# FFN down-projections: the weight slots of two output chunks interleaved

## What is computed

```python
D_FF = 2816
def conv_ffn(h, w_up, conv_w, conv_b, w_down):
    u = h @ w_up                      # 512 x 1024 by 1024 x 5632
    u = causal_conv3(u) + conv_b
    a, b = u[..., :D_FF], u[..., D_FF:]
    return (jax.nn.silu(a) * b) @ w_down   # 512 x 2816 by 2816 x 1024
x = x + conv_ffn(rms_norm(x, ffn_norm_g[layer]), w_up[layer], ...)
```

## Time and profile before

| | |
|---|---|
| median of three runs | 1828.44 us |
| the profiled execution, its own time | 1827.0 us |
| its span | 1825.1 us |
| PE busy | 1801.2 us, 99% |
| POOL line 1220 (low parts), 136 times | 584.3 us |
| PE line 844 (down-projections), 1056 matmuls | 411.7 us of busy time |
| PE clock granted, mean | 0.998 |

### The profile page before, as it was taken

The page is one execution under the profiler, slowest core; times in us unless marked ns, Lnnn a source line. Parts: engine busy times, 40 slices in busy tenths (PEclk is TensorE's granted clock), DMA queues, the critical chain, the costliest instruction groups (busy, mean ns, idle before and its releaser), DMA issues.

```text
span 1825.1 us, 24602 instructions
## 1 busy us (share of the span) xinstructions
PE 1801.2 (99%) x9595; PEld 1468.0 (80%) x9595; DVE 916.9 (50%) x1300; ACT 733.8 (40%) x970; POOL 681.3 (37%) x227
## 2 busy tenths in 40 slices
PE   9999989999999999999999999999999999999998
PEld 7799868888888887667888888888877788888886
DVE  6366764555552116664555555235227734313564
ACT  5251163555554224653455555222225542221423
POOL 2225834444443442100444443443343344344432
PEclk9999999999999999999999999999999999999999
DMA  8542202322322231110222222323421122332221
GB/s 333 217 139 70 71 1 75 110 92 92 104 88 79 95 122 62 52 54 24 92 103 105 92 92 84 105 95 108 105 69 47 47 92 92 107 103 105 69 71 68
DMA packets 28763, 170.36 MB, mean 93 GB/s; under 512 B 3216, under 2 KB 5520, under 8 KB 12432
## 3 DMA queue, kind: packets, MB, share of 16 engines
q1 hardware_dynamic: 25152, 151.20, 24.2%
q10 hardware_dynamic: 3536, 18.09, 3.0%
HBM read 167.18 MB, written 2.10 MB: 93 GB/s over the span
## 4 chain that ended last, share of the span: by engine, by line
PE 80%; issue 11%; DVE 3%; POOL 3%; ACT 2%; DMA 0%; ACTq 0%; POOLq 0%; DVEq 0%; SPq 0%
PE ps L403 47%; PE ps L844 12%; POOL wlo L1220 3%; PE ps L423 1%; PE ps L1111 1%; PE ps L700 1%; PE ps L425 1%; PE ps L424 1%; PE ps L1094 1%; PE ps L559 1%; PE ps L561 1%; PE ps L560 1%; PE ps L1123 1%; PE ps L1122 1%; PE ps L1121 1%
## 5 line engine op out<-in xcount | busy, mean ns | idle before, releaser
L1220 POOL TENSOR_TENSOR wlo<-wraw,whi 128x2048 fp32r<-128x2048 f32 (+1 forms) x136 | 584.3, 4296 | 963.2 <-ACT whi L1336 939.5
L403 PE MATMUL ps<-hh,whi 128*128 128x512 f32 x1328 | 520.1, 392 | 0.8 <-DVE wq L2481 0.4
L403 PE MATMUL ps<-hh,wlo 128*128 128x512 f32 x1328 | 516.9, 389 | 0.0
L403 PE MATMUL ps<-hl,whi 128*128 128x512 f32 x1328 | 516.8, 389 | 0.0
L1336 ACT ACTIVATE whi<-wraw 128x2048 fp32r<-128x2048 f32 (+3 forms) x147 | 261.3, 1778 | 356.7 <-PE ps L403 285.1
L403 PEld LDWEIGHTS ps<-hh,whi 128*128 128x128 f32 x1328 | 249.3, 188 | 54.7 <-issue 2.5
L403 PEld LDWEIGHTS ps<-hh,wlo 128*128 128x128 f32 x1328 | 249.3, 188 | 52.0
L403 PEld LDWEIGHTS ps<-hl,whi 128*128 128x128 f32 x1328 | 249.4, 188 | 51.8 <-issue 0.5
L2221 DVE SCALAR_TENSOR_TENSOR scr<-ps,vec,scr 128x510 f32<-128x510 f32 (+1 forms) x176 | 120.2, 745 | 93.1 <-ACT scr L1560 93.1
L844 PE MATMUL ps<-gh,whi 128*128 128x512 f32 x352 | 137.7, 391 | 1.3 <-DVE gl L2236 1.3
L844 PE MATMUL ps<-gh,wlo 128*128 128x512 f32 x352 | 137.0, 389 | 0.0
(11 more groups left out here) (488 smaller groups left out, 2836.8 us busy)
## 6 DMA issues: line engine op xcount, KB each, us to landing
wraw<-in_w SPq DMA_DIRECT2D x62, 1024.0 KB, 4.9
wraw<-in_w0b SPq DMA_DIRECT2D x26, 1024.0 KB, 4.9
wraw<-in_w1o SPq DMA_DIRECT2D x26, 1024.0 KB, 4.9
wraw<-in_wd SPq DMA_DIRECT2D x32, 704.0 KB, 4.0
ada<-in_wada ACTq DMA_DIRECT2D x12, 1024.0 KB, 8.5
xtok<-in_x SPq DMA_DIRECT2D x4, 512.0 KB, 7.2
out<-ytok SPq DMA_DIRECT2D x4, 512.0 KB, 4.0
wraw<-in_w SPq DMA_DIRECT2D x3, 576.0 KB, 3.9
```

The source lines that it names most:

```text
L403: last = mm(o, l, r, start=(k == 0 and n == 0), stop=(k == K - 1 and n == 2))
L1220: nc.gpsimd.tensor_tensor(wlo[:, s % 2, 0:wd], wraw[:, s % 2, 0:wd], whi[:, s % 2, 0:wd].bitcast(F32), ALU.subtract).then_inc(lo_ready, 1)
```

## The change

The order of the slots within a pair of output chunks changes. Before: chunk A first half, chunk A second half, chunk B first half, chunk B second half. Now: A first, B first, A second, B second. The weights are laid out for it on the host (`down`). Both PSUM banks are open at once. Chunk A is complete after the third slot of the pair and no longer after the second; chunk B after the fourth, as before. DVE's wait and ACT's conversions are moved to match: `conv_upto(S + 2 * k + 3 - k % 2)` makes the conversion of one slot more before the wait for an even chunk.

```diff
             def down_pair(S_D, layer, i):
-                for n in range(2):
-                    s = S_D + 2 * n
-                    pe.wait_ge(emptied, 4 * i + (s - 2))
-                    for hf in range(2):
-                        pe.wait_ge(lo_ready, 4 * i + (s + hf + 1))
-                        if n == 0 and hf == 1:
+                for hf in range(2):
+                    for n in range(2):
+                        s = S_D + 2 * hf + n
+                        if hf == 0:
+                            pe.wait_ge(emptied, 4 * i + (S_D + 2 * n - 2))
+                        pe.wait_ge(lo_ready, 4 * i + (s + 1))
+                        if hf == 1 and n == 0:
                             pe.wait_ge(f_lo, 22 * layer + 22)
-                        par = (s + hf) % 2
                         for k in range(11):
                             for m, (a, b) in enumerate(((0, 0), (0, 1), (1, 0))):
-                                last = mm(ps[:, 4 + n, :], (whi, wlo)[a][:, par, k * P:(k + 1) * P],
+                                last = mm(ps[:, 4 + n, :], (whi, wlo)[a][:, s % 2, k * P:(k + 1) * P],
...
                     if between:
                         between(k, 0)
-                    conv_upto(S + 2 * k + 2)
+                    conv_upto(S + 2 * k + 3 - k % 2)
                     act.wait_ge(emptied, S + 2 * k + 2)
...
                 for k in range(8):
-                    empty(S + 2 * k + 1)
+                    empty(S + 2 * k + 2 - k % 2)
                     x = xT[:, k, :]
                     TT(x, x, ps[:, 4 + k % 2, :], ALU.add).then_inc(emptied, 2)
...
 def down(wm):
-    return np.ascontiguousarray(wm.reshape(2, 11, P, 8, P).transpose(3, 0, 2, 1, 4).reshape(16, P, DSLOT))
+    return np.ascontiguousarray(wm.reshape(2, 11, P, 4, 2, P).transpose(3, 0, 4, 2, 1, 5).reshape(16, P, DSLOT))
```

## The result

| | before | changed |
|---|---|---|
| median of 15 runs, us | 1827.32 | 1832.15 |
| the profiled execution, us | 1827.0 | 1831.87 |
| its span, us | 1825.1 | 1829.9 |
| PE clock granted, mean | 0.998 | 0.997 |

The ratio is 1.0027, with a 95% interval from 1.0020 to 1.0034. The forecast time, 1831.8, is 0.35 us off, but that closeness is partly luck: the kernel before came out at 1827.32 here, 1.1 us under the 1828.44 that the forecast was added to. The difference is the honest measure: 4.8 us measured, 3.5 forecast, and slower by over 0.2% was given 40%.

The account below looks back on a forecast made before the run. The prediction took TensorE to bound the kernel. Layer 0's +0.5 us and layer 1's +3.0 summed to +3.5, added to the median 1828.44 for a forecast given as 1831.8 us, range 1828.6 to 1834.8.

Parts of the forecast that it names:

- What bounds the kernel: Whole kernel: TensorE bounds it, so a change is worth what it adds to or takes from TensorE's standing time.
- Part 1: Slot 1 of each layer's down-projection: the wait for f_lo goes, gain 1.9 us (1.7 to 2.0).
- Part 2: Layer 0, slots 4 to 15: chunks ending back to back stay covered by 0.5 us before the limit, cost 0.
- Part 3: Layer 0, slot 16: its conversion stands behind chunk 6's work, so its low part is 1.42 us late (1.3 to 1.6).
- E: The start of DVE's addition of a finished chunk, the clock from which conversions and POOL's low parts were timed.
- the limit: E + 7.04: when POOL's low part must be ready; each us past it is one us of TensorE.
- Part 4: Layer 1, context work queued ahead of conversions: slot 8 0.2 us late, slot 12 2.08, slot 16 2.76, net 2.0.
- The three small waits: Layer 1, slots 11, 13 and 15: waits for low parts of weights go, gain 0.3 us.
- One sign: POOL's low part was to become the releaser of the first matmul after each stage: 1.4 us layer 0, 2.8 layer 1.
- The clock: Rival: a long TensorE standstill sends it to 1.2 GHz, +7.5 us each, 1839.4 with one such slot; 4%.
- The cover holds: Rival: waits for `gl` and the small ones go and nothing takes their place, 1826.2 us; 9%.
- partly late: Rival: sooner handovers or downstream waits leave half the lateness, +0.8 us, 1829.2 us; 12%.

Follow-up runs that it names:

- x2: The kernel before with only pair 0 of each down-projection interleaved, pairs 1 to 3 unchanged; lower time 1825.1 us, ratio 0.9991.
- x4: The changed kernel with 11 idle matmuls on TensorE filling the wait ahead of layer 1's slot 16; lower time 1830.15 us, ratio to before 1.0019.
- x6: The changed kernel with layer 1's slot 12 conversion put ahead of chunk 4's square and three context high parts; ratio to before 1.0013.
- x1: The changed kernel with every conversion ahead of the wait for the finished chunk and all chunk and context work; lower time 1825.2 us, ratio 0.9991.
- x7: The changed kernel with layer 1's slot 16 conversion ahead of chunk 6's square and the last two context high parts; lower time 1828.85 us, ratio 1.0012.
- x3: The kernel before in its own slot order, with only the conversions put ahead of the chunk work; lower time 1826.5 us, ratio 0.9998.
- x5: The changed kernel with layer 0's slot 16 conversion put ahead of chunk 6's high part and square; lower time 1830.1 us, ratio to before 1.0020.
- x8: The kernel before with pair 0 alone interleaved and the conversions ahead of the chunk work; median 1824.70 us, lower time 1824.6, ratio 0.9991.

## Why the prediction was right, and the one term that it lacked

- *What bounds the kernel* held for all but the clock. That a change is worth "exactly what it adds to or takes from TensorE's standing time" is true of 3.1 of the 4.8 us; the other 1.7 are TensorE at work at half the clock. Reading the slot from the distance of two additions (7.48 us) and not from the matmuls' durations is what made the lateness visible.
- *Part 1*, the wait for f_lo: 1.9 us forecast, 0.94 and 0.95 in the trace, and 1.9 us alone in x2. Right.
- *Part 2*, back-to-back chunks cost nothing while the cover is 0.5 us: no slot of layer 0 from 4 to 15 waits. Right.
- *Part 3*, slot 16 of layer 0: 1.42 forecast, 1.33 measured, with POOL's end at E + 8.43. Right; by that loss the limit was at E + 7.10 there. The 0.65 us that POOL was said to have ahead of the limit in the kernel before are 0.5 by the working's own figures (677.77 - 0.16 - 677.10); no term rests on it.
- *Part 4*: slot 12, 2.08 forecast and 2.1 measured. Slot 16 until its start, 2.76 and 2.64. The three small waits, 0.3, gone: 0.36 by the starts. Slot 8, 0.2 forecast and 0.25 measured. POOL ended at 1194.52, E + 7.72 with E = 1186.80, 0.07 later than worked out; less the limit of 7.04 and the grace of 0.43 that is the 0.25 us. The times that come back behind slot 16, 0.8, came back. One sign was read off wrongly in advance: the view names not POOL but DVE's `xT` (layer 0) and "issue" (layer 1) for the first matmul of slot 16, and only the starts, 0.1 us behind POOL's ends, tell that it is POOL. Slot 8 in the changed kernel, where it is 1.13 us from slot 7's last matmul to slot 8's second, and 0.89 in the kernel before:

```profile
1193.78 0.39 PE L844 MATMUL ps<-gh,wlo 128*128 128x512 f32 x1
1194.01 0.59 PE L1018 MATMUL ps<-csq,con 128*128 128x256 f32 x2
1194.57 0.50 PE L844 MATMUL ps<-gh,whi 128*128 128x512 f32 x1
1194.91 0.40 PE L844 MATMUL ps<-gl,whi 128*128 128x512 f32 x1
```

- *The clock.* This is the step that failed: the sum put it at nothing, and it cost 1.7 us. That is more than the whole distance between 3.5 and 4.8; the other terms together came out 0.4 us lower than forecast. As a rival I gave it 4% and priced it as a whole slot at half speed, 7.5 us. It fell in the profiled execution after the 2.6 us standstill and not after the one of 2.1, and lasted 3.4 us, which is 1.7 us. Chance and price were both wrong, in opposite directions. The argument against it ("7 us of gapless matmuls on either side") was none: the matmuls ahead of the standstill did not protect it. x4 shows that without the standstill there is no fall; x6, that the standstill alone does not make it certain. A fall with TensorE idle was in the trace of before as well, though in none of the rows: behind its last matmuls the granted clock is 0.80 from 1818 to 1820 us and then 0.50, where nothing is left for it to slow. And of the three times of before one, 1826.79, was 1.7 us under the other two, as one fall would have it. The Trainium skill ("TensorE: Matmul & The Clock Gate", Part 1) has it that activity releases the throttle; by that rule, the trace of x4 agrees, since matmuls that compute nothing of use keep the clock at 1.00.
- *The cover holds* and *partly late* are out: nothing was handed over sooner than worked out.
- DVE held up by POOL played no part in the sum, and rightly: it was off the path in the changed kernel. It decides what the repair is worth. x1 and x7 each lose 0.96 us to it ahead of slot 16, x6 0.4 at slot 13.
- The measured time is inside the stated range, and the terms that were worked out hold to 0.15 us. The range itself does not follow from its parts: the lower and upper ends of the terms add up to +2.5 and +5.4 (stated +2.4 and +5.3), and 1833.7 + 1.4 is 1835.1, not 1834.8. The total came out near 1831.8 because two misses nearly cancel: the change, put 1.3 us too low, and the base, 1.1 us too high. That is luck.

## What to carry to other kernels

An in-order queue that feeds the critical engine must be read as a queue: when a producer's event moves, ask of each instruction behind it in the same queue whether it had been free to run earlier, and add up to the consumer's limit. The reordering that takes a wait away is needed only where the wait is (pair 0), and done everywhere, with the conversions left behind the chunk's work, it cost 4.8 us where pair 0 alone brings 1.9. And where a change makes TensorE stand, add a fall of the clock (1.7 us here) as a case of its own, or fill the wait with idle matmuls. The traces give no length from which on it has to be feared: falls came with waits of 1.1 and 2.6 us, and none with those of 2.1.

## What the runs showed of the hardware

**Two groups of times in every kernel.** In the latent attention, around 820 us, TensorE waits 1.12 us for ACT. In some executions the clock falls there for 3.4 us, in others not. The profiled execution of before (1827.0, lower group) and that of x3 (1828.06, upper group), the same stretch of each:

```profile
820.00:824.00 4.00, 3.28 (x11) 1.43 (x11) 3.69 (x5) 1.21 (x5) 0.00 (x0) 1.00 0.00 0
```

```profile
820.00:824.00 4.00, 3.37 (x5) 1.58 (x6) 3.61 (x5) 1.13 (x4) 0.00 (x0) 0.57 0.00 0
```

The next longer wait, 1.0 us, ends at 827.18, when such a fall is over. The profiled executions of before, x1, x5, x7 and x8 belong to the lower groups and have no fall there; those of x2, x3, x4 and x6 belong to the upper ones and have it. So in the traces the groups are one fall of the clock apart; for the executions without a trace that is inferred from their times. No run filled this wait, so that it is what takes the clock is argued from x4 and not shown.

When the fall begins is not tied to the wait either. In x3 it begins at about 820.2, with TensorE idle until 820.63; in x2 at about 820.6, when TensorE has been back since 819.71. At slot 16 it begins 1.1 us after TensorE resumes in the changed kernel, and in x5 0.25 us before. x5, by stretches:

```profile
1257.00:1257.50 0.50, 0.00 (x0) 0.00 (x0) 0.50 (x1) 0.00 (x0) 0.50 (x1) 1.00 0.00 0
1257.50:1258.00 0.50, 0.29 (x1) 0.32 (x2) 0.50 (x1) 0.00 (x0) 0.11 (x1) 0.54 0.00 0
```

In the changed kernel the fall at slot 16 comes on top in its lower group too; none of its 15 runs is below 1831.6, where one without any fall would be near 1830.1. The same holds for the 9 runs of x5. In x6, whose down stage is 1.7 us shorter up to that place, three runs of 11 are where one without any fall would be. Its profiled execution has the standstill of slot 16 at the same length and, to 0.01 us, at the same time of the launch as that of the changed kernel, and no fall. So neither length nor time decides. What does stays open.

**DVE behind POOL.** A DVE step of 0.48 us took 4.83, and one of 0.35 took 3.20, when POOL had started just before. The addition `xT<-xT,ps`, which reads one operand from PSUM, took 0.68 to 0.69 us always, beside POOL or not. The changed kernel shows both within a microsecond, while POOL works on slot 16's low part (1254.68 to 1259.24): the addition takes its 0.69 us, and the sum of squares behind it, 0.69 us elsewhere and both operands in SBUF, takes 2.22.

```profile
1256.96 0.69 DVE L2248 TENSOR_TENSOR xT<-xT,ps 128x512 f32<-128x512 f32 x1 [3.71 <-PE ps L844]
1257.57 2.22 DVE L1894 TENSOR_TENSOR scr<-scr 128x512 f32<-128x512 f32 x1
```
